# A routed-expert stage: GpSimd waits for the result rows' table at the first scatter, and the second expert's rows are turned between the first expert's two halves

## What is computed

```python
    def expert(acc, xs):
        wg, wu, wd, cw = xs
        h = jax.nn.silu(t @ wg) * (t @ wu)
        return acc + (h * cw[:, None]) @ wd, None

    y, _ = lax.scan(expert, jnp.zeros_like(t), (w_gate, w_up, w_down, combine.T.astype(t.dtype)))
```

## Time and profile before

| | |
|---|---|
| median of three executions | 1711.64 us (1709.96 to 1711.88) |
| the profiled execution's own time | 1710.01 us, of which the trace spans 1708.1 us |
| PE busy in the span | 1460.9 us, 86% |
| DVE, ACT, POOL busy | 617.0, 385.8, 227.3 us |
| HBM read and written | 301.46 MB and 41.84 MB, 201 GB/s over the span |
| stage of experts in layer 0, first gather to last scatter | about 646 to 911 us |
| the same in layer 1 | about 1404 to 1669 us |

### The profile page before, as it was taken

One profiled execution on the slowest core, in us unless ns is written; L12 is line 12 of the kernel. 1 busy time (PEld: TensorE's weight loads), 2 busy tenths in 40 slices (PEclk: granted clock), 3 DMA queues, 4 the chain that ended last, 5 costly groups with the idle time before them and its releaser, 6 DMA issues. The chain is left out here.

```text
span 1708.1 us, 22914 instructions
## 1 busy us (share of the span) xinstructions
PE 1460.9 (86%) x9025; PEld 987.0 (58%) x9025; DVE 617.0 (36%) x1408; ACT 385.8 (23%) x1002; POOL 227.3 (13%) x227
## 2 busy tenths in 40 slices
PE   6999998999796967998883999999977958998890
PEld 3688864999673454554441666666564454554440
DVE  3455532555473041231112563555432141221114
ACT  2144242344233010110111203224322100111111
POOL 0000012011230001222212001001000002222213
PEclk9999998999796997998996999999979978999985
DMA  9813600000434555999995213104353176999974
GB/s 314 241 74 95 152 6 1 1 1 2 158 87 154 230 216 223 382 387 390 400 393 190 84 36 136 49 1 185 124 197 145 77 283 254 379 391 402 400 285 177
DMA packets 106934, 328.97 MB, mean 193 GB/s; under 512 B 19189, under 2 KB 58973, under 8 KB 81951
## 3 DMA queue, kind: packets, MB, share of 16 engines
q1 hardware_dynamic: 90546, 275.43, 43.7%
q0 software_dynamic: 15040, 47.74, 7.8%
q10 hardware_dynamic: 1248, 4.46, 0.6%
HBM read 301.46 MB, written 41.84 MB: 201 GB/s over the span
## 5 line engine op out<-in xcount | busy, mean ns | idle before, releaser
L1960 PE MATMUL pp<-ring,uT 128*64 128x256 f32 x1728 | 230.6, 410 | 33.9 <-issue 24.0
L1960 PEld LDWEIGHTS pp<-ring,uT 128*64 128x64 f32 x1728 | 124.2, 141 | 130.9 <-issue 65.2
L564 PE MATMUL pp<-uT,ring 128*128 128x272 f32 x576 | 136.5, 396 | 0.9 <-PEq L359 0.9
L564 PEld LDWEIGHTS pp<-uT,ring 128*128 128x128 f32 x576 | 109.0, 192 | 22.7 <-issue 1.0
L1642 PE MATMUL pp<-ring,uT 128*128 128x512 f32 x256 | 114.4, 610 | 4.2 <-PEq L135 4.2
L1981 PE MATMUL pp<-ring,uT 128*64 128x512 f32 x432 | 103.4, 600 | 1.2 <-ACT uT L2011 1.2
L2005 ACT ACTIVATE uT<-pp 128x128 f32<-128x128 f32 x64 | 17.8, 277 | 381.8 <-PE pp L1960 381.8
L1999 DVE COPY uT<-pp 128x128 f32<-128x128 f32 x64 | 18.7, 292 | 233.9 <-PE pp L1970 233.9
L2136 POOL DMA_INDIRECT expert_rows<-uT,row_of_slot x64 | 64.7, 1010 | 248.2 <-ACT uT L2011 244.4
L1642 PEld LDWEIGHTS pp<-ring,uT 128*128 128x128 f32 x256 | 50.0, 196 | 67.5 <-issue 67.5
L1948 PE MATMUL pp<-consts 64*128 64x64 f32 x512 | 70.3, 282 | 18.5 <-DMA consts<-normed_rows,token_of_slot 18.5
(11 more groups left out here) (607 smaller groups left out, 2476.0 us busy)
## 6 DMA issues: line engine op xcount, KB each, us to landing
ring<-in_w_exp_gate SPq DMA_DIRECT2D x54, 1024.0 KB, 21.1
ring<-in_w_exp_up SPq DMA_DIRECT2D x54, 1024.0 KB, 27.4
ring<-in_w_exp_down SPq DMA_DIRECT2D x54, 1024.0 KB, 27.3
scaled_rows<-in_w_exp_gate SPq DMA_DIRECT2D x10, 1024.0 KB, 25.2
scaled_rows<-in_w_exp_up SPq DMA_DIRECT2D x10, 1024.0 KB, 29.5
ring<-in_w_in_a SPq DMA_DIRECT2D x3, 3072.0 KB, 12.6
expert_rows<-zero_rows SPq DMA_DIRECT2D x4, 2048.0 KB
scaled_rows<-in_w_exp_down SPq DMA_DIRECT2D x10, 512.0 KB, 22.8
```

Source lines behind the costliest of these rows:

```text
L564: TE.matmul(pp[n % 2][:, at], w[:, j, ct * P:(ct + 1) * P], uT[:, j, t], start=(j == 0), stop=(j == DJ - 1))
L1960: ins = TE.matmul(pp[0][q * SLOTS:(q + 1) * SLOTS, b * 512:b * 512 + 2 * P], xT[b][:, j, :], w[:, :, j, q, :], start=(j == 0), stop=(j == ...
```

## The change

Two moves, both at the head of the stage of experts, in each layer.

```diff
@@ POOL @@
                         pool.wait_ge(s_t, 1)
                         for e in range(ROWS_IN):
                             gather(e)
-                        pool.wait_ge(s_t, 2)
                         for e in range(ROWS_IN, NE):
                             gather(e)
+                            if e == ROWS_IN + 2:
+                                pool.wait_ge(s_t, 2)
                             if e >= ROWS_IN + 2:
                                 scatter(e - ROWS_IN - 2)
@@ PE @@
                         rank_tokens(pe)
                         turn(pe, main, 0, 0, 0)
                         gate_up(pe, main, 0, 0, 0, 0)
+                        turn(pe, main, 1, 1, 0)
                         gate_up(pe, main, 0, 0, 0, 1)
-                        turn(pe, main, 1, 1, 0)
                         with pe.Fori(0, loops) as i:
```

## The result

The changed kernel takes 1699.71 us (median of six executions, 1695.76 to 1701.67), the kernel before 1711.76 us (median of six): a ratio of 0.994, 95% interval 0.9921 to 0.9959. That is 12 us faster. The forecast was 1699.4 us in a range of 1694.5 to 1705.5.

What follows compares the result with a forecast made beforehand. The weight stream on full DMA engines was taken to bound the stage; 6.1 + 5.85 - 2 x 1.09 + 2 x 1.2 = 12.2 us off the median 1711.64 gave 1699.4 us, range 1694.5 to 1705.5.

Steps and rivals of the forecast that it cites:

- What bounds: Stage of experts: once running, it goes at the weight stream's pace; head gains are read as idle DMA time.
- Rival A: Stage of experts: PE sets the pace, so its gains of 6.6 + 8.1 = 14.7 us count, 1697 us; chance 0.14.
- Gather 2: Stage head: issued at 651.5 instead of 661.1, landing before PE wants it; PE's waits of 4.33 and 4.44 us go.
- The table's wait behind gather 4: POOL, stage head: the moved wait for the result rows' table costs nothing, with some 2 us of cover.
- Fetch 7: Expert 7's gate and up fetch, stage head: issued 5.4 us behind expert 6's instead of 13, closing the DMA hole.
- The sum: Both layers' stage heads: 6.1 + 5.85 - 2 x 1.09 + 2 x 1.2 = 12.2 us gained, passed through undiminished.
- The turn: Between expert 0's halves: removes PE's copy waits of 0.98 and 0.97 us, delays expert 6's fetch 1.09 us per layer.
- B: Rival: part given back by the clock in layer 1's tail or a late gather; gain 4 to 10 us; chance 0.20.
- the late gather: Stage head: gather 3 meets expert 6's fetch and takes 8.5 us; 2 us are left, every us beyond is lost.
- C: Rival: the hole is filled but something behind the stage, or the last experts, hides it: 1708 to 1715; chance 0.07.
- D: Rival, stage head: the turn breaks PE's work and the clock stays low, starving the stream: above 1715; chance 0.04.

Runs made afterwards that it cites:

- the turn alone: The kernel before with only expert 1's turn moved between expert 0's halves, the third gather still waiting for the table: 1711.66 us, ratio 1.001.
- the wait alone: The kernel before with only POOL's wait for the result rows' table moved to the first scatter: 1698.81 us, ratio 0.9937; again 1699.41 us, ratio 0.994.

## Why the prediction was right, and where it was not

- **What bounds.** That the stage goes at the pace of the weight stream, and that the gain is to be read in idle DMA time at its head, was the step on which all rests. Holding fetch 7 shows it: PE as early as in the changed kernel, the median of before. At the head, where the engines are idle, fetch 7 issued 6.95 us later in each layer (12.2 us behind fetch 6 instead of 5.2) cost 8 to 9 us of the median. Rival A (PE's 14.7 us) falls with it. PE also runs out of fetched weights earlier, as forecast: its first stand in the loop begins 117 us after the first turn, before 124.
- **Gather 2.** Issued 0.8 us after expert 0's turn, landed 2.7 us later by the trace, wanted 8.7 us after the issue: no wait, as worked out. The 4.8 us that I took for a light queue was not one: that gather went 3.6 us behind fetch 6, into full engines (the weight queue alone took 112% of them from 661 to 661.5 us). The misreading did no harm here, where gather 2 met idle engines; it spoiled the forecast for the turn alone. The table's wait behind gather 4 cost nothing; the first scatter (672.71) waited for ACT's result.
- **Fetch 7.** Forecast 5.4 us behind fetch 6, measured 5.2 in both layers.
- **The sum.** 12.2 us of idle time were forecast (6.2 and 6.0, by the terms given), 12.6 measured (6.6 and 6.0), and the median moved by 12.0. That they agree so closely is in part luck: the interval of the ratio reaches from 7 to 13.5 us. The profiled stages gave 15.3 us. Layer 1 gave 2.7 us more than its idle time, and the clock in its tail is of just that size: expert 29 took 10.7 us at the low clock in the trace of before, and 8.2 us in that of the changed kernel (1632.03 to 1640.19):

```profile
1632.03 3.36 PE L1960 MATMUL pp<-scaled_rows,uT 128*64 128x256 f32 x16 [3.25 <-issue]
...
1640.19 1.98 PE L1960 MATMUL pp<-ring,uT 128*64 128x256 f32 x16
```

These 2.6 us can differ from one execution to the next, so they are not to be counted as a gain of the change: in its two traces the wait alone has a clock of 0.68 in this place (16 us that begin 32 us ahead of the last scatter) and of 1.00.

```profile
1630.79:1646.79 16.00, 12.68 (x65) 6.33 (x63) 1.40 (x4) 1.47 (x3) 1.01 (x1) 0.68 0.95 379
1629.58:1645.58 16.00, 11.94 (x84) 6.31 (x80) 1.56 (x4) 1.75 (x4) 2.83 (x3) 1.00 0.98 394
```

- **The turn.** Here the working was right in the main and its weight was not seen. I listed the 0.98 us on PE that it removes and the 1.09 us by which it delays fetch 6, and did not say that the two nearly cancel on the stream: the wait alone gives the same time within the noise, the turn alone gives none. The delay was smaller in layer 0 than I had it: fetch 6 came 6.71 us after the first `gate_up` began, before 5.99.
- **The other rivals.** Of B, the late gather did not come with the whole change, but it is just what undid the turn alone. C and D did not happen. In layer 0 of the changed kernel's trace the first half ran at the granted clock of 0.50 (3.68 us for 16 matmuls); the clock was still 0.50 up to 662 us and 0.94 in the us behind it, as the turn ended, and the next 32 matmuls took 3.85 us.

## What to carry to other kernels

Where a stage runs at the pace of a prefetch stream, look at its head for the time in which the transfer engines are idle, and ask which instruction releases the next transfer; an order written by hand can put a wait there for something that is needed only later. A wait belongs at its first user, since whatever stands behind it on an in-order engine waits as well, here a gather, the tensor engine and in the end the weights. An edit that shortens a wait on the compute engine pays only as far as it moves the transfers, and one that cuts transfers finer to start earlier is to be tried only where the engines are idle.

## What I had not expected of the hardware

In these traces a gather of 64 rows of 4 KB is late by where it stands to a bulk fetch: with idle engines it landed 2.7 us after its issue, PE had its rows after 5.0 us where it followed 3.6 us behind the 2 MiB of fetch 6, and after 7.5 and 8.1 us where it followed 0.15 and 0.6 us behind. Cutting 1 MiB weight transfers in two took 0.5 to 0.8% off the rate of a full stream, in one trace. And the spread between executions of one program was 13 us of 1700 for the changed kernel on one chip (1689.42 to 1702.79) and 15 us with fetch 7 held (1700.19 to 1715.1); in the pair of traces above, 9.8 us lay in a stretch of unchanged code in which the granted clock differed.
